# Two transformer blocks with an expert layer on one core: an earlier first search, tiles parked in the gathers' rows, another order in the mixer

## The chip, the cores and the metric

The program runs on one core of a Trainium2 chip. Five engines work side by side, each through its own list of instructions in order: TensorE (PE in the profile), VectorE (DVE), ScalarE (ACT), GpSimd (POOL), and SyncE (SP), which issues most of the transfers. They wait for each other on semaphores only. The metric is device time in microseconds of one execution, and less is better. All numbers are float32.

## The reference, cut to what matters

256 tokens of width 1024 go through two blocks. The first is a mixer (attention, and a gated linear scan in both directions), an expert layer and a small gate layer. The second is a mixer (attention, and an mLSTM) and a feed-forward layer. Most of the time lies in the expert layer:

```python
q = (ht @ w_q).reshape(T, PEER_HEADS, 2, PEER_DKEY // 2)
s = jnp.einsum('thpc,hpnc->thpn', q, sub_keys)
v1, i1 = lax.top_k(s[:, :, 0], K)                 # K = 16 of 128 keys
v2, i2 = lax.top_k(s[:, :, 1], K)
cand = (v1[..., :, None] + v2[..., None, :]).reshape(T, PEER_HEADS, K * K)
top_s, pos = lax.top_k(cand, K)                   # 16 pairs of 8 heads: 128 experts a token
idx = jnp.take_along_axis(cand_idx, pos, axis=-1) # cand_idx = i1 * 128 + i2
g = jax.nn.softmax(top_s, axis=-1)
a = jnp.einsum('thkd,td->thk', jnp.take(u, idx, axis=0), x)
w = jax.nn.gelu(a) * g
out = jnp.einsum('thk,thkd->td', w, jnp.take(v, idx, axis=0))
```

## The kernel before, in words

The 256 tokens are two blocks (b = 0, 1) of 128, one token per partition. Weights come in tiles of 2 MB through a ring of three slots (`wring`); the list `TILES` sets their order, and SP loads tile n when the product of tile n-3 is done, in that order, one after the other (L444). Products go to eight PSUM banks by the list `PLAN`. `reserved` takes a bank that another engine has emptied, `begin` counts the product in, and `wait_product` and `wait_moved` are the waits on a product and on its bank being emptied.

The order of work is written out by hand for each engine. What the change touches, in order of time:

- **Start.** SP loads block 0 of x, two small tensors, the first weight tile (`in_hf`) and block 1 of x. PE turns block 0 of the normed x (L503) and multiplies it with the whole tile (`by_block`, L596), then does the same for block 1.
- **Before the expert layer.** PE lifts both branches (`lifted`, L664: `up_att` 0 to 3, `up_hg` 0 to 3) with the transposes `g_OT` between them (L676), then makes the output product: `out0` and `out1` are the two halves of 512 columns, each for both blocks (`merged_out` L693, `by_rows` L514). DVE adds them to x (`out_added`, L1711). When block 0 is whole, ACT takes its squares (`rms`) and DVE scales it (L1440), PE turns it (`turn_query`), ACT moves it, and PE makes the query for the first head (`first_query`, L740) and its scores with the keys (`first_score`, L748); ACT copies the scores to SBUF.
- **The search.** DVE finds the 16 best of 128 keys on either side (`best_keys`), makes the 256 sums (`candidates`), finds the best 16 (`best_pairs`) and their expert numbers (`located`, L1779 writes `idx_t`). `route_first(0)` does it for the first head, `route_first(1)` for the second; later pairs of heads are cut in pieces and put between the batches by `ROUTE_AFTER`.
- **The gathers.** POOL issues one indirect DMA per slot k of 128 slots and two blocks, 256 in all (L1397). Each brings for 128 tokens one expert's row of u and of v, 8 KB a token, 1.05 MB, into one of ten rows of a ring (`pair_ring`). Gather k goes to row (k + 1) mod 10, and from k = 10 on it waits until slot k - 10 is used. Row r lies at columns 2048 r of the buffer `big`, which the mixer used before.
- **The batches.** Four slots make a batch m. DVE takes the dot products with u (`dots`, L1824), ACT the tanh of the gelu and then four diagonal matrices with the weights (`spread`, L1196), PE adds them times v (`experts`, L771). Queries of later heads are made one piece a batch (`dealt`, L715); `QUERY_FROM` says which from which batch on.
- **The mixer of the second block** (1028 to 1082 us). PE makes the scores of block 0 and 1 (`d_S`, L903), the mLSTM's `m_cols`, `m_M`, `m_S` and `m_num` (L945), the output gates (`in2_og`), the transposes of the probabilities (`d_PT`, L956) and the attended values (`d_Y`, L967). DVE and ACT work in between: `probs` and `og_tanh` on ACT, `attention_normed`, `mlstm_divided` and `mlstm_out` on DVE, which also sums the adaptive weights (`ada_sums`) where it has time.

## Time and profile before

| | us |
|---|---|
| median of 3 runs | 1347.11 (1346.61 to 1347.72) |
| the profiled execution's own time | 1346.32 |
| its span, first to last instruction | 1344.4 |
| PE busy | 1220.1 (91%) |
| DVE busy | 789.9 (59%) |
| ACT busy | 229.8 (17%) |
| POOL busy | 319.9 (24%) |

The span falls into three parts. Up to some 260 us PE works nearly without a pause. From there to some 933 us the 256 gathers run, and in most slices of the page the 16 DMA engines move about 420 GB/s. The rest is PE again.
### The profile page before, as it was taken

What the parts mean: (1) busy time and instruction counts of PE and PEld (TensorE: products, weight loads), DVE (VectorE), ACT (ScalarE), POOL (GpSimd) and SP (SyncE); (2) the same over time, 40 slices, a digit from 0 to 9 for tenths busy, and PEclk for the clock granted to TensorE, in tenths of its full rate; (3) what the DMA queues carried; (4) which work ended last, traced back from release to release, by engine and by line L of the source; (5) the groups of instructions that cost most, each with busy time, mean ns of one, the idle gap of its engine ahead of it and who ended that gap; (6) DMA issues with size and microseconds to landing.
All of it is one profiled execution on the core that took longest, in us unless ns stands there. A gap on an engine that the chain in (4) does not pass through costs nothing.

```text
span 1344.4 us, 12494 instructions
## 1 busy us (share of the span) xinstructions
PE 1220.1 (91%) x4454; PEld 735.7 (55%) x4454; DVE 789.9 (59%) x1878; ACT 229.8 (17%) x592; POOL 319.9 (24%) x276
## 2 busy tenths in 40 slices
PE   8999999978988989678889896888999999999998
PEld 7767987654544544233333342333457559888743
DVE  3766874569675877777786775656357752220101
ACT  2133210121111111112211112112201421000000
POOL 0100000124544444354545444452000000000000
PEclk9999999989989999888899999999999999999999
DMA  8441656399999999999999999999656634575540
GB/s 308 149 165 63 250 203 227 143 396 399 395 420 421 422 414 420 417 421 403 419 422 420 422 395 421 421 421 389 243 204 242 206 115 147 190 238 146 188 156 31
DMA packets 92732, 399.16 MB, mean 297 GB/s; under 512 B 6464, under 2 KB 9920, under 8 KB 59776
## 3 DMA queue, kind: packets, MB, share of 16 engines
q0 software_dynamic: 37440, 270.30, 48.9%
q1 hardware_dynamic: 55232, 128.08, 27.1%
q8 instruction: 36, 0.59, 0.2%
q14 instruction: 24, 0.20, 0.0%
HBM read 397.30 MB, written 1.06 MB: 296 GB/s over the span
## 4 chain that ended last, share of the span: by engine, by line
PE 57%; DMA 23%; DVE 14%; ACT 2%; issue 2%; POOL 1%; SPq 0%; DVEq 0%; ACTq 0%
DMA big<-in_peer_uv,idx_t 20%; PE ps L526 16%; PE ps L771 11%; PE ps L514 10%; DVE big L1824 6%; PE ps L1030 6%; PE ps L596 3%; PE ps L992 2%; PE ps L664 2%; DMA wring<-in_w_in 1%; PE ps L715 1%; DMA wring<-in_peer_wq 1%; PE ps L693 1%; PE ps L574 1%; POOL big L1397 1%
## 5 line engine op out<-in xcount | busy, mean ns | idle before, releaser
L771 PE MATMUL ps<-big,rows 128*128 128x512 f32 x1024 | 488.8, 634 | 101.4 <-ACT rows L1196 101.3
L771 PEld LDWEIGHTS ps<-big,rows 128*128 128x128 f32 x1024 | 202.6, 203 | 370.2 <-issue 370.2
L1397 POOL DMA_INDIRECT big<-in_peer_uv,idx_t x256 | 308.5, 1205 | 392.2 <-PE ps L771 332.7
L1824 DVE CUSTOM_DVE_ANT_0 big<-big 128x1024 f32<-128x1024 f32 x256 | 307.8, 1224 | 142.0 <-DMA big<-in_peer_uv,idx_t 138.9
L526 PE MATMUL ps<-big,wring 128*128 128x256 f32 x1088 | 236.8, 379 | 0.0
L526 PEld LDWEIGHTS ps<-big,wring 128*128 128x128 f32 x1088 | 206.0, 190 | 28.0 <-issue 0.5
L514 PE MATMUL ps<-wring,big 128*128 128x512 f32 (+1 forms) x336 | 140.0, 573 | 0.0
L514 PEld LDWEIGHTS ps<-wring,big 128*128 128x128 f32 x336 | 63.0, 190 | 70.5 <-issue 68.2
L1190 ACT ACTIVATE small<-small 128x4 f32<-128x4 f32 (+2 forms) x68 | 14.0, 205 | 500.6 <-DVE small L1829 491.7
L1196 ACT ACTIVATE rows<-const,small 128x128 f32<-128x128 f32 x256 | 82.2, 390 | 20.3 <-DVE small L1833 18.8
L1030 PE MATMUL ps<-wring,big 128*128 128x512 f32 x176 | 75.7, 592 | 0.0
L715 PEld LDWEIGHTS ps<-big,wring 128*128 128x128 f32 x448 | 55.4, 199 | 17.2 <-issue 9.1
L715 PE MATMUL ps<-big,wring 128*128 128x128 f32 x448 | 55.9, 282 | 7.9 <-DMA wring<-in_peer_wq 7.9
L1030 PEld LDWEIGHTS ps<-wring,big 128*128 128x128 f32 x176 | 33.4, 190 | 41.7 <-issue 41.6
L2058 DVE TENSOR_TENSOR big<-big,ps 128x512 f32<-128x512 f32 x11 | 7.6, 688 | 82.1 <-PE ps L526 74.8
L2026 DVE SCALAR_TENSOR_TENSOR big<-ps,big 128x512 f32<-128x512 f32 x8 | 5.5, 692 | 84.4 <-PE ps L1030 70.6
L1377 POOL TENSOR_TENSOR small<-small,lane 128x8 f32<-128x8 f32 x2 | 1.3, 626 | 222.9 <-DVE small L1496 222.9
L1496 DVE CUSTOM_DVE_ANT_0 wring<-wring,c_row 128x1024 f32<-128x1024 f32 x40 | 47.1, 1219 | 6.1 <-DMA wring<-in_w_ada 4.9
L596 PE MATMUL ps<-big,wring 128*128 128x128 f32 x384 | 45.1, 281 | 3.9 <-DMA wring<-in_w_in 2.9
L1075 ACT ACTIVATE big<-ps 128x512 f32<-128x512 f32 (+1 forms) x58 | 31.5, 576 | 93.3 <-PE ps L514 23.6
L596 PEld LDWEIGHTS ps<-big,wring 128*128 128x128 f32 x384 | 44.7, 197 | 4.8 <-issue 3.6
L1363 POOL DMA_DIRECT2D rows<-in_norm_ffn x1 | 0.7, 692 | 130.6 <-DVE big L1671 130.6
(246 smaller groups left out, 932.4 us busy)
## 6 DMA issues: line engine op xcount, KB each, us to landing
wring<-in_w_in SPq DMA_DIRECT2D x17, 2048.0 KB, 10.2
wring<-in_w_ada SPq DMA_DIRECT2D x10, 2048.0 KB, 7.7
wring<-in_w_gate SPq DMA_DIRECT2D x5, 2048.0 KB, 7.9
wring<-in_w_up SPq DMA_DIRECT2D x5, 2048.0 KB, 13.1
wring<-in_w_down SPq DMA_DIRECT2D x5, 2048.0 KB, 8.2
wring<-in_w_out SPq DMA_DIRECT2D x4, 2048.0 KB, 9.0
wring<-in_peer_wq SPq DMA_DIRECT2D x4, 2048.0 KB, 7.9
big<-in_peer_uv,idx_t POOLq DMA_INDIRECT x256
```

What stands on the lines that cost most here:

```text
L514: last = nc.tensor.matmul(o[:, 0:w], lhs[:, c, b * P:(b + 1) * P], wt[:, c, c0:c0 + w], start=(c == 0), stop=(c == k - 1))
L526: last = nc.tensor.matmul(o[:, c2 * S:(c2 + 1) * S], wt[:, c, n0:n0 + P], src[:, c, :], start=(c == 0), stop=(c == KD - 1))
L596: last = nc.tensor.matmul(o[:, c2 * S + b * P:c2 * S + (b + 1) * P], wt[:, c, n0:n0 + P], src[:, c, b * P:(b + 1) * P], start=(c == 0), st ...
L664: last = nc.tensor.matmul(o[:, c2 * S:(c2 + 1) * S], wt[:, c, n0:n0 + P], lhs[:, c, :], start=(c == 0), stop=(c == 3))
L715: last = nc.tensor.matmul(o[:, n * P:(n + 1) * P], wt[:, c, n * P:(n + 1) * P], h2T[b][:, c, :], start=(c == 0), stop=(c == KD - 1))
L771: last = nc.tensor.matmul(banks[h], diag[:, k % DIAGS, :], v_part[:, ring_at(k), h * 512:(h + 1) * 512], start=False, stop=(k % SLOTS == S ...
L1030: last = nc.tensor.matmul(o, gT[:, f, b * P:(b + 1) * P], wt[:, c, h * 512:(h + 1) * 512], start=(f == 0), stop=(f == FC - 1))
L1075: nc.scalar.activation(dst, bank(name, n) if src is None else src, ACT.Copy).then_inc(emptied(*name), 1)
L1196: nc.scalar.activation(diag[:, k % DIAGS, :], ident, ACT.Copy, scale=w_now[:, at_w:at_w + 1])\
L1397: pool.indirect_dma_start(pair_ring[:, ring_at(k), :], None, a["peer_uv"], bass.IndirectOffsetOnAxis(idx_t[:, k:k + 1], 0))\
L1496: last = nc.vector.tensor_tensor_reduce(w[:, c, :], w[:, c, :], c_row[:, :], 1.0, 0.0, ALU.mult, ALU.add, to[:, c:c + 1])
L1824: nc.vector.tensor_tensor_reduce(u_part[:, ring_at(k), :], u_part[:, ring_at(k), :], h_t[:, b, :], 1.0, 0.0, ALU.mult, ALU.add, a_dot[:, i ...
```

## The change

Nothing of the computation changes but its order and places.

- The first weight tile comes in two transfers (chunks 0 to 3, then 4 to 7 of the rows). PE starts on the first with column pieces 0 and 2. ACT no longer waits for the small tensor `lane` before the first squares.
- `up_att` 2 is multiplied before the transposes `g_OT` instead of after them.
- The second output tile (`out1`) and the second query tile (`peer_q1`, for block 0) are loaded into rows 6, 7 and rows 8, 9 of the gathers' ring. `peer_q1` is loaded a second time, into `wring`, for block 1. Gathers 5, 6 and 9 of the first round now wait until `out1` is done, and gathers 7 and 8 until `peer_q1` of block 0 is done. Tile `peer_q3` comes earlier in the list. The gain row of the norm moves from `rows2` to `big`.
- The scaled block 0 is handed to PE in halves. PE's order around the first query is new (below).
- The first head's search is made in two steps: the eight best pairs from the eight best keys on each side, read from PSUM, with an index step on both sides at once; then the other eight. The second head's search comes after the first batch of dots, and the second pair of heads one batch later. Scaling block 1 comes after that, too.
- `peer_q1` for block 0 precedes the first batch on PE, `peer_q2` for block 0 and the turning of block 1 follow it.
- In the mixer PE makes `m_cols` and `m_M` before the scores of block 1, `in2_og` 0 after `m_S`, and `in2_og` 1 after `m_num`; DVE and ACT follow in a like order.

TensorE between `out1` of block 0 and the first batch, before. L693 is `out0` of block 1, L503 the turning of block 0, L740 the first query, L748 the first head's scores, L514 `out1` of block 1, L715 both queries `peer_q1` and `peer_q2`, L726 their scores, L771 the first batch.

```order
L693 MATMUL ps<-wring,big 128x512 x5
L503 MATMUL ps<-const,big 128x128 x8
L693 MATMUL ps<-wring,big 128x512 x3
L740 MATMUL ps<-big,wring 128x128 x24
L748 MATMUL ps<-big 128x128 x2
L740 MATMUL ps<-big,wring 128x128 x8
L748 MATMUL ps<-big 128x128 x2
L514 MATMUL ps<-wring,big 128x512 x8
L715 MATMUL ps<-big,wring 128x128 x64
L726 MATMUL ps<-big 128x128 x4
L778 MATMUL ps<-x_t,const 128x512 x2
L771 MATMUL ps<-big,rows 128x512 x8
```

The same place in the changed kernel. L722 is the output product (from `big` where it is `out1`), L773 the turning, L782 the first query, L790 its scores. After these rows come 32 matmuls of `peer_q1` (L749), its scores and the batch; those of `peer_q2` follow the batch.

```order
L722 MATMUL ps<-wring,big 128x512 x4
L773 MATMUL ps<-const,big 128x128 x8
L722 MATMUL ps<-wring,big 128x512
L782 MATMUL ps<-big,wring 128x128 x16
L722 MATMUL ps<-wring,big 128x512
L790 MATMUL ps<-big 128x128 x2
L722 MATMUL ps<-wring,big 128x512 x2
L782 MATMUL ps<-big,wring 128x128 x16
L722 MATMUL ps<-big 128x512
L790 MATMUL ps<-big 128x128 x2
L722 MATMUL ps<-big 128x512 x7
L749 MATMUL ps<-big 128x128 x32
```

Half of the first query (16 matmuls) and two chunks of `out0` have gone behind the first scores.

VectorE after the two sums of block 0 are added, before: the search of the first head for the 16 best keys on both sides (rows 201 to 210 on this engine).

```order
L1724 MAX big<-big 128x8
L1725 MATCH_REPLACE rows<-big 128x128
L1726 MAX_INDEX big<-big 128x8
L1727 MAX big<-rows 128x8
L1728 MAX_INDEX big<-big,rows 128x8
L1724 MAX big<-big 128x8
L1725 MATCH_REPLACE rows<-big 128x128
L1726 MAX_INDEX big<-big 128x8
L1727 MAX big<-rows 128x8
L1728 MAX_INDEX big<-big,rows 128x8
```

The changed kernel from its fourth row of the search on, as far as the first eight expert numbers (L1865, row 216; the search begins at row 202).

```order
L1881 MAX_INDEX big<-big,ps 128x8
L1883 CAST big<-big 128x2x8
L1869 TENSOR_TENSOR big<-big 128x8x8
L1885 MAX big<-big 128x8
L1886 MAX_INDEX big<-big 128x8
L1857 TENSOR_SCALAR big<-big 128x8
L1858 TENSOR_SCALAR big<-big 128x8
L1859 CAST big<-big 128x2x8
L1861 TENSOR_TENSOR big<-const,big 128x128
L1863 TENSOR_TENSOR big<-big 128x128
L1864 TENSOR_REDUCE big<-big 128x2x8
L1865 SCALAR_TENSOR_TENSOR idx_t<-big 128x8
```

Before, `idx_t` is row 229, so the search is 29 instructions long. Now it is 15 long, all on eight values a side, with no MATCH_REPLACE.

ScalarE in the mixer, from the last exponentials of the mLSTM's decays, before (L1308 is `og_tanh`, L1049 a table load, L1075 a copy out of PSUM, L1056 and L1057 the norm's Ln and Exp).

```order
L1320 ACTIVATE big<-big,small 128x128
L1308 ACTIVATE big<-ps 128x512
L1049 ACT_TABLE_LOAD
L1075 ACTIVATE big<-ps 128x512 x2
L1056 ACTIVATE lnms<-ms 128x4
L1057 ACTIVATE rstd<-lnms 128x4
L1075 ACTIVATE big<-ps 128x512 x4
L1056 ACTIVATE lnms<-ms 128x4
```

The same place now (L1357 the exponentials of block 1's probabilities, L1361 `og_tanh`, L1098 and L1101 table loads, L1127 a copy).

```order
L1371 ACTIVATE big<-big,small 128x128
L1357 ACTIVATE big,small<-big,small 128x256 x8
L1361 ACTIVATE big<-ps 128x512
L1098 ACT_TABLE_LOAD
L1105 ACTIVATE lnms<-ms 128x4
L1106 ACTIVATE rstd<-lnms 128x4
L1105 ACTIVATE lnms<-ms 128x4
L1106 ACTIVATE rstd<-lnms 128x4
L1101 ACT_TABLE_LOAD
L1361 ACTIVATE big<-ps 128x512
L1127 ACTIVATE big<-ps 128x512 x6
L1098 ACT_TABLE_LOAD
```

Both norms' Ln and Exp now stand ahead of `og_tanh` 1 and of all six copies, between two table loads.

The diff, cut to its core:

```diff
-    starts = {(0, 1): 0, (0, 2): 6, (0, 3): 14, (1, 0): 20, (1, 1): 26, (1, 2): 34, (1, 3): 42}
+    starts = {(0, 1): 1, (0, 2): 6, (0, 3): 14, (1, 0): 20, (1, 1): 26, (1, 2): 34, (1, 3): 42}
...
-QUERY_FROM = {1: (1, 0), 5: (1, 1), 9: (0, 3), 14: (1, 2), 19: (1, 3)}
+QUERY_FROM = {1: (1, 0), 5: (0, 3), 9: (1, 2), 14: (1, 1), 19: (1, 3)}
...
-    t += [(f"out{i}", KD, 512, "w_out", 0, 512 * i) for i in range(2)]
-    t += [(f"peer_q{i}", KD, 512, "peer_wq", 0, 512 * i) for i in range(4)]
+    t += [("out0", KD, 512, "w_out", 0, 0)]
+    t += [(f"peer_q{i}", KD, 512, "peer_wq", 0, 512 * i) for i in (0, 2, 3, 1)]
...
-    p += [("in_g3", 1), ("g_O", 0), ("g_O", 1), ("up_att", 0), ("up_att", 1), ("g_OT", 0), ("g_OT", 1)]
-    p += [("up_att", 2), ("up_att", 3), ("up_hg", 0), ("up_hg", 1), ("up_hg", 2), ("up_hg", 3)]
+    p += [("in_g3", 1), ("g_O", 0), ("g_O", 1), ("up_att", 0), ("up_att", 1), ("up_att", 2), ("g_OT", 0), ("g_OT", 1)]
+    p += [("up_att", 3), ("up_hg", 0), ("up_hg", 1), ("up_hg", 2), ("up_hg", 3)]
     p += [("out0", 0), ("out1", 0)]
-    p += half("n2T", 0) + [("out0", 1), ("peer_q0", 0, 0), ("keys", 0, 0, 0), ("peer_q0", 0, 1), ("keys", 0, 0, 1), ("out1", 1)]
-    p += [("peer_q1", 0), ("peer_q2", 0), ("keys", 0, 1), ("keys", 0, 2)] + half("n2T", 1)
+    p += half("n2T", 0) + [("peer_q0", 0, 0), ("keys", 0, 0, 0), ("out0", 1), ("peer_q0", 0, 1), ("keys", 0, 0, 1)]
+    p += [("out1", 1), ("peer_q1", 0), ("keys", 0, 1), ("peer_q2", 0)] + half("n2T", 1) + [("keys", 0, 2)]
...
-    p += [("d_S", 1, i, g) for i in range(2) for g in range(2)]
-    p += [("m_cols",), ("m_M", 0), ("m_M", 1)] + [("m_S", h) for h in range(GH)] + [("in2_og", 1)]
-    p += [("m_num", b, i) for b in range(NB) for i in range(2)]
+    p += [("d_S", 0, i, g) for i in range(2) for g in range(2)] + [("in2_vm", 1), ("m_cols",), ("m_M", 0), ("m_M", 1)]
+    p += [("d_S", 1, i, g) for i in range(2) for g in range(2)] + [("m_S", h) for h in range(GH)] + [("in2_og", 0)]
+    p += [("m_num", b, i) for b in range(NB) for i in range(2)] + [("in2_og", 1)]
...
+                if n == 0:
+                    t = wring[:, 0:TILE].rearrange("p (c n) -> p c n", c=k)
+                    rows_ = a[src][0:D, :].rearrange("(c p) n -> p c n", p=P)[:, :, c0:c0 + w]
+                    sp.dma_start(t[:, 0:4], rows_[:, 0:4]).then_inc(first_half, 16)
+                    sp.dma_start(t[:, 4:8], rows_[:, 4:8]).then_inc(tile_landed[0], 16)
+                    sp.dma_start(x[:, 1, :], a["x"][P:S, :]).then_inc(x_landed[1], 16)
...
+                if name == "out0":
+                    wait_product(sp, "g_O", 1)
+                    sp.dma_start(out1_home, a["w_out"].rearrange("(c p) n -> p c n", p=P)[:, :, 512:1024])\
+                      .then_inc(out1_landed, 16)
+                if name == "peer_q0":
+                    wait_product(sp, "up_hg", 3)
+                    sp.dma_start(q1_home, a["peer_wq"].rearrange("(c p) n -> p c n", p=P)[:, :, 512:1024])\
+                      .then_inc(q1_landed, 16)
...
+            pe.wait_ge(first_half, 16)
+            for pieces, halves in (((0, 2), (0, 1)), ((1,), (0, 1)), ((3,), (0, 1))):
+                for c0 in halves:
+                    if c0:
+                        tile("in_hf", KD, 512)
+                    for n in pieces:
+                        o = ps[:, BANK[("in_hf", n // 2)], n % 2 * S:n % 2 * S + P]
+                        for c in range(4 * c0, 4 * c0 + 4):
+                            nc.tensor.matmul(o, first_tile[:, c, n * P:(n + 1) * P], hT[:, c, 0:P], start=(c == 0),
+                                             stop=(c == KD - 1), skip_group_check=True)
...
+            lifted("up_att", 2)
...
-            lifted("up_att", 2)
...
-                wt = tile(f"out{i}", KD, 512)
+                if i:
+                    pe.wait_ge(out1_landed, 16)
+                wt = out1_home if i else tile("out0", KD, 512)
...
+                if (name, b) == ("peer_q1", 0):
+                    pe.wait_ge(q1_landed, 16)
+                    wt = q1_home
...
             reserved("out0", 1)
-            merged_out(0, 1, range(0, 5))
-            turn_query(0)
-            begin("out0", 1)
-            merged_out(0, 1, range(5, 8)).then_inc(product_done, 1)
+            merged_out(0, 1, range(0, 4))
+            for h in range(2):
+                if h == 0:
+                    pe.wait_ge(h_half, 1)
+                else:
+                    pe.wait_ge(h_ready, 3)
+                o = begin("n2T", 0, h)
+                for c in range(4):
+                    last = nc.tensor.transpose(o[:, c * P:(c + 1) * P], h_t[:, 0, (4 * h + c) * P:(4 * h + c + 1) * P],
+                                               ident)
+                last.then_inc(product_done, 1)
+            merged_out(0, 1, range(4, 5))
             wait_turned("n2T", [0])
...
             o = begin("peer_q0", 0, 0)
             first_query(0, o)
             first_query(1, o).then_inc(product_done, 1)
-            first_query(2, reserved("peer_q0", 0, 1))
+            merged_out(0, 1, range(5, 6))
             pe.wait_ge(keys_landed, 16)
             first_score(0)
-            first_query(3, begin("peer_q0", 0, 1)).then_inc(product_done, 1)
+            begin("out0", 1)
+            merged_out(0, 1, range(6, 8)).then_inc(product_done, 1)
+            o = begin("peer_q0", 0, 1)
+            first_query(2, o)
+            first_query(3, o).then_inc(product_done, 1)
+            reserved("out1", 1)
+            merged_out(1, 1, range(0, 1))
             first_score(1)
-            by_rows("out1", hT, blocks=[1])
+            begin("out1", 1)
+            merged_out(1, 1, range(1, 8)).then_inc(product_done, 1)
...
+            score(0, 1)
             experts(0, banks)
+            query("peer_q2", 0)
+            turn_query(1)
             score(0, 2)
-            turn_query(1)
...
+                squares = at(rows2, 0, D) if (k, b) == (1, 1) else h_t[:, b, :]
+                link(nc.scalar.activation(squares, x[:, b, :], ACT.Square, accum_out=stat(ms, n)))
+                if (k, b) == (0, 0):
+                    act.wait_ge(lane_landed, 16)
...
+                    move(sc[(0, 0)][:, c, :], "keys", 0, 0, 1,
+                         src=bank(("keys", 0, 0, 1), 2 * P).rearrange("p (c t) -> p c t", c=2))
             best(0)
             act.wait_ge(x_whole, 2)
...
-            best(1)
...
+            probs(1)
+            og_tanh(0)
+            log_and_exp()
+            rsqrt(M_STAT)
+            rsqrt(M_STAT + 1)
+            exp_and_tanh()
             og_tanh(1)
...
-            wait_moved(pool, "g_O", 0)
+            pool.wait_ge(g_out, 1)
...
                 elif k % (SLOTS // PAIRS) == 0:
-                    pool.wait_ge(indexed, k // (SLOTS // PAIRS) + (2 if k else 1))
-                if ring_at(k) == 0 and k < RING:
+                    pool.wait_ge(indexed, k // (SLOTS // PAIRS) + (3 if k else 1))
+                if k < RING and ring_at(k) in (0, 6, 7):
                     wait_product(pool, "out1", 1)
+                if k < RING and ring_at(k) in (8, 9):
+                    wait_product(pool, "peer_q1", 0)
...
             out_added(1, 0)
             dve.wait_ge(gain_landed, 16)
-            scale(1, 0, gain)
-            out_added(0, 1)
+            dve.wait_ge(rstd_ready, norm_stat(1, 0) + 1)
+            for h in range(2):
+                c = slice(h * 512, (h + 1) * 512)
+                stt(h_t[:, 0, c], x[:, 0, c], stat(rstd, norm_stat(1, 0)), gain[:, c], ALU.mult, ALU.mult)\
+                    .then_inc(h_ready if h else h_half, 1)
...
-            def route_first(h):
...
+            def eight_located(first, width):
+
+                c = slice(first, first + 8)
+                ts(pos_u[:, 0, c], best_i[:, 0, c], 4, None, ALU.logical_shift_right)
...
+                h4 = hot[:, 0:2 * 8 * width].rearrange("p (s n k) -> p s n k", s=2, n=8)
...
+                link(tt(h4, h4, top_f[:, 0, :, 0:width].unsqueeze(2).to_broadcast([P, 2, 8, width]), ALU.mult))
...
+                stt(idx_t[:, c], part[:, 0, c], float(NKEYS), part[:, 1, c], ALU.mult, ALU.add).then_inc(indexed, 1)
...
+            def route_eight():
+
+                wait_product(dve, "keys", 0, 0, 0)
+                for n in range(2):
+                    link(nc.vector.max(top_v[:, n, low], first_scores[:, n, :]))
+                    last = nc.vector.max_index(top_i[:, n, low], top_v[:, n, low], first_scores[:, n, :])
+                link(last)
+                nc.vector.tensor_copy(top_f[:, 0, :, low], top_i[:, 0:2, low])
+                link(pair_sums(cand[:, 0], low, low))
+                link(nc.vector.max(best_v[:, 0, low], first_sums))
+                link(nc.vector.max_index(best_i[:, 0, low], best_v[:, 0, low], first_sums))
+                eight_located(0, 8)
...
+            route_eight()
+            out_added(0, 1)
+            route_eight_more()
+            weighed(0, 0, 0, 1, 0)
             out_added(1, 1)
-            route_first(1)
-            scale(1, 1, gain)
             for m in range(HALF_BATCHES):
                 dots(m)
                 if m == 0:
+                    route_second()
+                    scale(1, 1, gain)
+                if m == 1:
```

## Rows read from the trace of the kernel before

**Rows 1.** The page, parts 2 (GB/s in 40 slices) and 4 (the chain).

```profile
GB/s 308 149 165 63 250 203 227 143 396 399 395 420 421 422 414 420 417 421 403 419 422 420 422 395 421 421 421 389 243 204 242 206 115 147 190 238 146 188 156 31
...
DMA big<-in_peer_uv,idx_t 20%; PE ps L526 16%; PE ps L771 11%; PE ps L514 10%; DVE big L1824 6%; PE ps L1030 6%; PE ps L596 3%; PE ps L992 2%; PE ps L664 2%; DMA wring<-in_w_in 1%; PE ps L715 1%; DMA wring<-in_peer_wq 1%; PE ps L693 1%; PE ps L574 1%; POOL big L1397 1%
```

**Rows 2.** Stretches, by clock: us; busy and (instructions) per engine; PEclk, DMA share, GB/s.

```profile
260.00:270.00 10.00, 7.72 (x66) 7.29 (x64) 9.07 (x41) 1.65 (x4) 6.69 (x7) 1.00 0.83 312
290.00:320.00 30.00, 25.91 (x95) 14.15 (x93) 27.07 (x91) 5.55 (x17) 14.59 (x12) 1.00 0.98 375
330.00:340.00 10.00, 8.99 (x20) 4.09 (x21) 8.31 (x21) 2.92 (x10) 4.78 (x3) 0.83 0.87 338
```

**Rows 3.** Transfers from 200 to 262 us: GB/s in 40 slices of 1.55 us.

```profile
GB/s 0 0 11 0 0 0 53 217 414 385 408 391 389 388 384 387 388 386 381 325 20 0 0 0 0 0 0 0 0 16 296 410 399 233 0 11 0 5 0 22
```

**Rows 4.** Timeline of DVE: start us, us, line, operation, count, [idle before <-releaser].

```profile
239.83 1.28 DVE L1440 SCALAR_TENSOR_TENSOR big<-x_t,rstd,rows 128x1024 f32<-128x1024 f32 x1 [1.91 <-ACT rstd L1071]
...
251.19 0.29 DVE L1724 MAX8 big<-big 128x8 f32<-128x128 f32 x1 [5.53 <-ACT big L1075]
...
260.84 0.17 DVE L1779 SCALAR_TENSOR_TENSOR idx_t<-big 128x16 uint32<-128x16 f32 x1
...
278.45 1.23 DVE L1824 CUSTOM_DVE_ANT_0 big<-big 128x1024 f32<-128x1024 f32 x1 [1.25 <-DMA big<-in_peer_uv,idx_t]
```

**Rows 5.** Timeline of POOL: the gathers' issues.

```profile
261.30 1.03 POOL L1397 DMA_INDIRECT big<-in_peer_uv,idx_t  x1 [36.73 <-DVE idx_t L1779]
...
291.50 0.94 POOL L1397 DMA_INDIRECT big<-in_peer_uv,idx_t  x1 [17.20 <-PE ps L771]
```

**Rows 6.** Timeline of PE from `up_hg` to the first batches.

```profile
209.48 13.98 PE L664 MATMUL ps<-big 128*128 128x256 f32 x64
...
237.03 4.45 PE L693 MATMUL ps<-wring,big 128*128 128x512 f32 x10
...
260.42 7.31 PE L715 MATMUL ps<-big,wring 128*128 128x128 f32 x64
275.67 9.60 PE L715 MATMUL ps<-big,wring 128*128 128x128 f32 x64 [7.94 <-DMA wring<-in_peer_wq]
...
289.27 7.11 PE L771 MATMUL ps<-big,rows 128*128 128x512 f32 x16 [1.39 <-ACT rows L1196]
...
299.81 7.10 PE L771 MATMUL ps<-big,rows 128*128 128x512 f32 x16 [1.67 <-ACT rows L1196]
```

**Rows 7.** Timeline of ACT ahead of the first batch.

```profile
286.69 0.21 ACT L1185 ACTIVATE big<-big 128x16 f32<-128x16 f32 x1
286.92 1.28 ACT L1052 ACT_TABLE_LOAD   x1
288.21 0.20 ACT L1190 ACTIVATE small<-small 128x4 f32<-128x4 f32 x1
```

**Rows 8.** Waits of PE, 0 to 262 us: who, for whom, us in total, times, longest.

```profile
PE ps L676 <- DVE big L1679: 1.7, 2, 1.4
```

**Rows 9.** Timeline of DVE at the start.

```profile
7.75 1.29 DVE L1447 TENSOR_TENSOR big<-ps,lane 128x512 f32<-128x512 f32 x2 [0.93 <-PE ps L503]
```

**Rows 10.** Timeline of PE at the start.

```profile
11.03 8.82 PE L596 MATMUL ps<-big,wring 128*128 128x128 f32 x64 [2.88 <-DMA wring<-in_w_in]
...
21.71 7.38 PE L596 MATMUL ps<-big,wring 128*128 128x128 f32 x64 [0.99 <-DVE big L1447]
```

**Rows 11.** Timeline of PE in the mixer.

```profile
1071.17 4.59 PE L945 MATMUL ps<-big 128*128 128x129 f32 x24 [2.07 <-DVE big L1989]
...
1079.85 1.99 PE L967 MATMUL ps<-big 128*64 128x128 f32 x32 [0.45 <-ACT big L1075]
```

**Rows 12.** Timeline of DVE in the mixer.

```profile
1056.31 2.48 DVE L1957 SCALAR_TENSOR_TENSOR big<-ps,const 128x512 f32<-128x512 f32 x4 [3.30 <-PE ps L903]
...
1079.08 0.17 DVE L1425 TENSOR_SCALAR ms<-ms 128x4 f32<-128x4 f32 x1
```

**Rows 13.** Timeline of ACT in the mixer.

```profile
1077.55 2.04 ACT L1075 ACTIVATE big<-ps 128x512 f32<-128x512 f32 x4
```

116 lines of the change are left out of this document (74 added, 42 removed).

## The prediction

> **What bounds the kernel now.** I read the page's slices and chain first, then the waits of PE ahead of the gathers, then the timelines around the places that the change touches.
>
> The slices show the gathers' part: from slice 9 to slice 28 the transfers run at 389 to 422 GB/s, and the chain that ended last has 20% of its length in gathers [rows 1]. 256 gathers of 1.05 MB at 420 GB/s take 2.50 us each, 640 us together. While they saturate, no engine's work counts; what counts is when the stream starts and how often it is interrupted. It starts late: the first gather is issued at 261.30 [rows 5], and the stretch 260 to 270 moves 312 GB/s, so the full rate begins about 2.6 us into it, at 262.6. Two later stretches show where it is interrupted: against 420 GB/s, 290 to 320 loses 3.2 us (375 of 420 over 30 us) and 330 to 340 loses 2.0 (338 over 10), 5.2 together [rows 2]. Before the gathers PE runs nearly without pause, so its order sets when the scores come; and after them PE is the bound again, with waits of 2.07 and 0.45 us in the mixer [rows 11].
>
> The profiled execution took 1346.32 us, 0.8 less than the median. The sum is made against it, and 0.8 is added at the end.
>
> **First tile in halves.** PE waits 2.88 us for the tile, from 8.15 to 11.03 [rows 10]. The input that it multiplies has been written only at 7.75 + 1.29 = 9.04 [rows 9]. With the first half landed by then, PE starts at 9.2: 1.8 us. The first 64 matmuls also take 8.82 us where the second 64 take 7.38 [rows 10], which I put down to a lower clock behind the pause; with a pause of 1 us instead of 2.9 it may go, another 1.1 to 1.4. Bounds 1.8 and 3.3; I take −2.9, near the row 21.71, because the pause that is left is as long as the 0.99 us ahead of that row, behind which the rate was full. PE is the chain's engine up to the output product, so this carries through.
> The Trainium skill ("TensorE: Matmul & The Clock Gate", "What's actually happening") calls the throttled rate the default, which activity lifts. By it the start after any pause this early would be slow again, and this term would be −1.8; row 11.03 agrees, row 21.71 speaks for the other.
>
> **`up_att` 2 first.** PE waits twice, 1.7 us in all, for the gated output before `g_OT` [rows 8]. The moved product is one of those that L664 makes: four of them take 13.98 us from 209.48 [rows 6], so one takes 3.5, and it covers both waits: −1.7, bounds 0 and −1.7.
>
> **The gathers' start.** This is the large term. In the frame of before:
> - PE: chunks of the output product cost 4.45 / 5 = 0.89 us (ten rows in the trace are five matmuls) from 237.03 [rows 6]. After four chunks PE is at 240.5. DVE's scaling began at 239.83 and took 1.28 [rows 4]; its first half ends at 240.5, the second at 241.1. The eight transposes end at 241.9, the fifth chunk covers ACT's copy (242.7). Two of four query pieces (four pieces of L715 take 7.31 from 260.42, so a piece 1.83 [rows 6]) end at 246.4, one chunk at 247.2, the score product at 247.8. Before, three pieces, the copy and the copy of the scores let DVE begin at 251.19 [rows 4]. Now it reads PSUM: it begins at 247.95.
> - DVE: the old search runs from 251.19 to 260.84 + 0.17 [rows 4], 9.8 us for 29 instructions, 0.34 each. The new has 15; at that mean 5.1, but none is wider than 128 values where before half were 256 wide. A MAX over 128 is 0.29 [rows 4]; at 0.28 it is 4.2. I take 4.2: the indices are there at 252.15 instead of 261.0, the first gather is issued at 252.4 instead of 261.3: 8.9 earlier.
> - Transfers: tile `peer_q3` now takes the slot of `out0`, which is free when its last two chunks for block 1 are done, at 247.8 + 1.8 = 249.6, so the queues are busy from about 250.8 instead of 262.6: 11.8 us earlier. Both kernels then have ten gathers and one tile in front of them, 12.6 MB or 30 us, before a row has to come free.
> - Waits of POOL: gathers 0 to 4 use rows 1 to 5, free at once. Gathers 5 and 6 wait for `out1` of block 1, which PE ends at 260.7 (from 247.8: two chunks, two pieces, eight chunks of `out1`, the second scores 0.4); 7 and 8 for `peer_q1`, 7.3 later at 268.0. From 250.8 on, the tile (5 us) and gathers 0 to 4 (12.5) keep the queues busy until 268.3, two more until 273.3, so nothing runs dry. Behind POOL's wait stand only gathers.
> - The first rows come free when batch 0 has been multiplied. Gather 3 lands some 17 us after its first issue (278.45 − 1.25 − 261.3 + 0.9, [rows 4, 5]), less 2.5 for the tile that now is ahead of them instead of between: 266.6. Its dots end at 268, ACT has copies until 270.5, then a table load of 1.28 [rows 7], the tanh and four diagonals 1.9: PE starts batch 0 at 273.0. Before it started at 289.27, after 7.94 us of waiting for `peer_q2` in the middle [rows 6]. So the eleventh gather can be issued at about 276 instead of 291.5 [rows 5].
> - But batch 1 has the second head's search in front of it on DVE: 9.8 us plus 1.3 of scaling, all behind the first dots. Its diagonals come at 289.5, and PE starts it at 290 (before 299.81 [rows 6]). Between the slots freed by batch 0 and those of batch 1 the queues run dry for about 3.4 us, at 291 to 295, and some 1.2 us more goes in small gaps: 4.6 in all, against 5.2 before.
>
> The gain is 11.8 + 0.6 = 12.4 us. After 340 both are at the full rate, where the slot of a batch is freed well ahead. Bounds: by DVE and PE alone (batch 1 is 9.8 us earlier, not 12.4) −9; by the first issue with both earlier terms included, 8.9 + 4.6 = 13.5. The cost of the second `peer_q1` load, 5 us of transfer, is nothing net: a tile of 2.1 MB that was loaded ahead of the gathers' start (`peer_q3` now, `out1` and `peer_q1` before they start) has left the stretch. If that cover fails it costs 5 us.
> What is late next in this stretch is DVE, with both searches.
>
> **Loads before it.** Before, the transfers ahead of `out0` run from about 210 us (slice 7) to 230 at 388 GB/s [rows 3]: keys, `out0`, `out1` and `peer_q0`, 1 + 3 x 2.1 MB = 7.3 MB. The same four tensors come now, `out1` into another place and behind the same `out0`; only `peer_q1` is new, after `up_hg` 3 at 223.5 [rows 6], needed at 260. `out1` is needed at 230 and is third of the four: (1 + 4.2) MB at 388 GB/s is 13.4 us, landed near 224. 6 us to spare: nothing.
>
> **The mixer.** PE makes `m_M` first, so DVE waits less than its 3.30 us before the second score block [rows 12] and begins it at about 1053. Its row of work from 1056.31 to 1079.08 + 0.17 [rows 12] is 22.9 us; 2.3 of `m_M` and 1.5 of waits leave it, two adaptive sums of 1.15 come in. It ends at 1074.6. But ACT now does both norms' Ln and Exp (0.45) and a second table load (1.28, [rows 7]) ahead of `og_tanh` 1 (0.6) and the copies of d_PT, whose last four take 2.04 us from 1077.55 [rows 13]. So these begin at 1078.1 and end at 1080.3, and the attended values, at 1079.85 before [rows 11], start at 1080.4: +0.5. PE is idle longer ahead of it (4 us, before 2.07 [rows 11]), so the products behind may run slower, 0 to 1.2. I take +1.0, bounds −0.5 and +2.2.
> The Trainium skill ("ScalarE: Activation LUTs", "What ACT_TABLE_LOAD costs") adds to each load of about 1283 ns a drain of about 1380 ns. Here the row before the load ends at 286.90, the load starts at 286.92, and the next activation at 288.21 [rows 7]: no drain is seen. By the page's rule this term would be +2.4 and the total an estimated 1332.5; I go by the row.
>
> **The sum.** −2.9 − 1.7 − 12.4 + 1.0 = −16.0: 1330.3 for a profiled execution, 1331.1 for the median.
>
> **The rivals.**
> - Consumption sets the early pace. DVE has to do 11 us of search behind the first dots and PE two queries between batches 0 and 1; if each is a few us longer than I have it, the ring of ten is full and the queues stand. Then the stage gains what batch 1 gains, 9.8, less a delay of the first dots by about one gather (2.5 us) that shares the queues with the tile: 7 in place of 12.4: 1331.1 + 5.4 = 1336.5. For it: the interruptions are all in 290 to 340 [rows 2], where batches 0 to 4 are. Against: the ring holds 30 us of transfer.
> - Only the front gains. The gathers start earlier but their end is set by something after the first stretch, so that the stage ends where it did: −2.9 − 1.7 + 1.0 leave 1343.5. For it: three slices between 12 and 27 show under 415 GB/s [rows 1]. Against: the rest are at 420 and leave no slack to give back.
> - The gain is larger. The gaps of 290 to 340 vanish altogether, another 4.6: 1326.5.
> - Slower than before: the tile `out1` lands late. The queues bring the four tensors and, from 223.5, `peer_q1`, at less than I have, and PE stands in front of the second half of the output product; the scores, the search and the whole stream of gathers move by as much. It decides from the point at which that delay eats the 16 us, `out1` landing at 246 in the frame of before. If the queues gave no more than the 143 GB/s of slice 8 [rows 1] and shared it evenly among the 7.3 MB, the last would land 51 us after 208, at 259, 29 late: 1360. For it: slices 5 to 8 show 143 to 250 GB/s [rows 1]. Against: those are what was asked for; when four tensors were asked for at once it was 388 [rows 3].
>
> **How the numbers follow.** Forecast (1327.5 to 1334.5) 0.60; consumption 0.20 (1334.5 to 1340); only the front 0.07; larger 0.08; slower, the late tile, 0.05. The range 1326.5 to 1338.5 holds the first, most of the second and half of the fourth, 0.8. A measurement of this kernel tells 0.2%, 2.7 us, from no change: faster takes all of the first, second and fourth and half of the third, 0.92; same 0.03; slower 0.05.
>
> **What would show it.** PE's first products start near 9.2 at full clock; no wait at `g_OT`; the first MAX near 243 and the first gather near 248 (both 4.6 earlier than the frame above); `out1` and `peer_q1` without a wait; batch 0 on PE near 268, batch 1 near 285; a gap in the transfers of about 3 us in front of batch 1's slots; the rate of 420 GB/s from 335 on, and 256 gathers over 16 us earlier; the attended values 0.5 us later against their stage. The prediction is wrong if batch 1 comes after 290, if the queues stand more than 8 us in total before 335, or if PE waits for `out1`.

## The result, and the profile after

| | before | changed |
|---|---|---|
| median of 4 runs, us | 1347.41 (1346.61 to 1349.61) | 1332.34 (1332.32 to 1332.90) |
| the profiled execution's own time | 1346.32 | 1332.32 |
| its span | 1344.4 | 1330.5 |

The ratio is 0.9885 (95% interval 0.9869 to 0.9902): faster by 1.15%. 1331.1 was forecast. Measured again later, beside other runs of before, the same kernel gave 0.9880 (0.9861 to 0.9899). The kernel before had medians from 1347.41 to 1350.37 us in the four series of this document, so kernels of different series are compared by their ratios. One execution among those below stands apart, 2851.89 us in the kernel with the earlier table load: its ratio leaves it out, and the median of its other four is 1331.44.

The page of the changed kernel, its GB/s in 40 slices and its chain, answering to [rows 1]:

```profile
GB/s 312 184 133 64 253 200 321 291 373 406 418 421 420 421 423 415 416 420 410 418 421 422 397 405 422 421 420 339 231 190 252 206 127 156 191 223 143 190 158 32
...
DMA big<-in_peer_uv,idx_t 20%; PE ps L543 18%; PE ps L818 12%; PE ps L531 8%; DVE big L1941 6%; PE ps L1079 6%; PE ps L613 3%; PE ps L691 2%; PE ps L722 2%; PE ps L1041 2%; PE ps L749 2%; PE ps L591 1%; POOL big L1454 1%; DMA wring<-in_w_in 1%; ACT rows L1247 1%
```

The stream of gathers is as full as before and its share of the chain is still 20%. It begins and ends about half a slice earlier: the first gather falls into slice 8 in both kernels (291 GB/s, before 143). Slice 7 (321 GB/s, before 227) holds weight tiles, of which two more now come there: SP issues `peer_q1` at 218.01 and `peer_q2` at 218.42.

PE at the start, for [rows 10]:

```profile
8.85 7.66 PE L628 MATMUL ps<-big,wring 128*128 128x128 f32 x64 [0.99 <-DVE big L1504]
...
18.37 7.38 PE L613 MATMUL ps<-big,wring 128*128 128x128 f32 x64 [0.99 <-DVE big L1504]
```

The pause is 0.99 us instead of 2.88, the 64 products take 7.66 instead of 8.82, and the second run starts at 18.37 instead of 21.71: 3.34 us. PE at `g_OT` (L704, the old L676), which no longer waits for DVE, at `up_hg`, at batches 0 and 1 and behind the last batch, for [rows 8 and 6]:

```profile
199.68 1.04 PE L704 MATMUL ps<-const,big 128*128 128x128 f32 x8
...
204.00 13.98 PE L691 MATMUL ps<-big 128*128 128x256 f32 x64
...
267.68 7.10 PE L818 MATMUL ps<-big,rows 128*128 128x512 f32 x16 [3.00 <-ACT rows L1247]
...
285.35 7.11 PE L818 MATMUL ps<-big,rows 128*128 128x512 f32 x16 [1.57 <-ACT rows L1247]
...
927.40 3.67 PE L898 MATMUL ps<-wring,big 128*128 128x512 f32 x8 [0.51 <-DMA wring<-in_w_in]
```

`up_hg` starts at 204.00 (before 209.48), 5.48 earlier: 3.34 from the start and 2.14 from the two waits at `g_OT`. The first search on DVE, for [rows 4]:

```profile
242.37 0.30 DVE L1880 MAX8 big<-ps 128x8 f32<-128x128 f32 x1 [6.60 <-PE ps L790]
...
244.04 0.43 DVE L1885 MAX8 big<-big 128x8 f32<-128x256 f32 x1
...
246.49 0.17 DVE L1865 SCALAR_TENSOR_TENSOR idx_t<-big 128x8 uint32<-128x8 f32 x1
```

The search takes 4.29 us from 242.37 to 246.66, where it was 9.8. One of its rows is 256 wide (L1885, the `cand` buffer whose unused part is filled with a large negative number), which I had not seen. POOL, for [rows 5]:

```profile
246.95 1.03 POOL L1454 DMA_INDIRECT big<-in_peer_uv,idx_t  x1 [27.86 <-DVE idx_t L1865]
...
255.21 0.94 POOL L1454 DMA_INDIRECT big<-in_peer_uv,idx_t  x1 [2.24 <-PE ps L722]
...
262.35 0.94 POOL L1454 DMA_INDIRECT big<-in_peer_uv,idx_t  x1 [4.40 <-PE ps L749]
...
287.58 0.94 POOL L1454 DMA_INDIRECT big<-in_peer_uv,idx_t  x1 [11.58 <-PE ps L818]
```

The first issue is 14.35 us earlier. The two waits for the parked tiles (2.24 and 4.40 us) stop nothing: the transfers run at the full rate from 250 to 280, and stand only in the next stretch, for [rows 2]:

```profile
250.00:280.00 30.00, 27.00 (x153) 19.38 (x152) 22.38 (x74) 6.04 (x14) 12.23 (x12) 1.00 1.02 421
280.00:290.00 10.00, 8.43 (x45) 5.73 (x44) 8.34 (x33) 3.54 (x9) 1.64 (x2) 1.00 0.72 278
290.00:310.00 20.00, 18.32 (x66) 9.99 (x65) 18.63 (x61) 2.96 (x10) 10.28 (x9) 1.00 0.99 391
```

Against 420 GB/s, 280 to 290 loses 3.4 us, 290 to 310 another 1.4: 4.8, where 4.6 was forecast. ACT ahead of batch 0 and of batch 1, for [rows 7]:

```profile
265.34 1.28 ACT L1101 ACT_TABLE_LOAD   x1
266.63 0.20 ACT L1241 ACTIVATE small<-small 128x4 f32<-128x4 f32 x1
...
283.81 0.60 ACT L1127 ACTIVATE big<-ps 128x512 f32<-128x512 f32 x1 [0.27 <-PE ps L760]
284.31 0.20 ACT L1241 ACTIVATE small<-small 128x4 f32<-128x4 f32 x1
```

And the mixer, PE and then ACT, for [rows 11 and 13]:

```profile
1012.06 1.91 PE L926 MATMUL ps<-const,big 128*128 128x128 f32 x16
...
1061.89 5.83 PE L1016 MATMUL ps<-big 128*64 128x128 f32 x48 [3.73 <-ACT big L1127]
...
1068.37 7.03 PE L1041 MATMUL ps<-wring,big 128*128 128x512 f32 x16
```

```profile
1058.46 0.20 ACT L1105 ACTIVATE lnms<-ms 128x4 f32<-128x4 f32 x1 [5.55 <-DVE ms L1482]
...
1058.92 1.28 ACT L1101 ACT_TABLE_LOAD   x1
...
1060.71 3.04 ACT L1127 ACTIVATE big<-ps 128x512 f32<-128x512 f32 x6
```

PE waits 3.73 us in one piece and then makes the attended values in 5.83 us; before they took 1.09 and 1.99. From the first transposes of the mixer (L926) to the output product (L1041) it is 56.3 us, before 54.0 (1028.26 to 1082.26).

The account, by the starts of rows that both kernels have: start of the kernel to the second run of 64 products −3.34; `g_OT` −2.14; from there to the end of the batches −10.9 (the product behind them starts at 927.40, before 943.76); from there to the mixer +0.2; the mixer +2.3. Together −13.9, the difference of the spans.

### The profile page after: what moved, and what is told of

Its sections match the earlier page's. It is cut to its first block, busy times and chain, and to the rows that moved or that the text cites. A ratio compares the mean times of both kernels' runs of the same rounds, so it can differ in the third digit from the quotient of the medians.

```text
span 1330.5 us, 12510 instructions
## 1 busy us (share of the span) xinstructions
PE 1211.0 (91%) x4454; PEld 730.4 (55%) x4454; DVE 791.2 (59%) x1886; ACT 231.9 (17%) x593; POOL 321.6 (24%) x276
## 4 chain that ended last, share of the span: by engine, by line
PE 60%; DMA 21%; DVE 14%; issue 2%; ACT 2%; POOL 1%; DVEq 0%; SPq 0%
DMA big<-in_peer_uv,idx_t 20%; PE ps L543 18%; PE ps L818 12%; PE ps L531 8%; DVE big L1941 6%; PE ps L1079 6%; PE ps L613 3%; PE ps L691 2%; PE ps L722 2%; PE ps L1041 2%; PE ps L749 2%; PE ps L591 1%; POOL big L1454 1%; DMA wring<-in_w_in 1%; ACT rows L1247 1%
## 5 line engine op out<-in xcount | busy, mean ns | idle before, releaser
L818 PE MATMUL ps<-big,rows 128*128 128x512 f32 x1024 | 482.4, 627 | 107.3 <-ACT rows L1247 107.2
L818 PEld LDWEIGHTS ps<-big,rows 128*128 128x128 f32 x1024 | 199.9, 200 | 371.8 <-issue 371.8
L543 PEld LDWEIGHTS ps<-big,wring 128*128 128x128 f32 x1088 | 206.0, 190 | 28.0 <-issue 0.5
L531 PE MATMUL ps<-wring,big 128*128 128x512 f32 (+1 forms) x304 | 126.0, 571 | 0.0
L1241 ACT ACTIVATE small<-small 128x4 f32<-128x4 f32 (+2 forms) x68 | 13.9, 205 | 502.3 <-DVE small L1946 502.3
L531 PEld LDWEIGHTS ps<-wring,big 128*128 128x128 f32 x304 | 57.0, 190 | 62.8 <-issue 61.0
L1079 PEld LDWEIGHTS ps<-wring,big 128*128 128x128 f32 x176 | 33.4, 190 | 41.7 <-issue 41.6
L749 PEld LDWEIGHTS ps<-big,wring 128*128 128x128 f32 x384 | 46.0, 192 | 9.1 <-issue 9.1
L749 PE MATMUL ps<-big,wring 128*128 128x128 f32 x384 | 46.3, 275 | 0.0
L1127 ACT ACTIVATE big<-ps 128x512 f32<-128x512 f32 (+1 forms) x57 | 31.0, 582 | 73.9 <-PE ps L531 23.8
L613 PE MATMUL ps<-big,wring 128*128 128x128 f32 x320 | 36.3, 275 | 1.0 <-DVE big L1504 1.0
L613 PEld LDWEIGHTS ps<-big,wring 128*128 128x128 f32 x320 | 36.0, 192 | 1.7 <-DVE big L1504 1.2
```

The lines of the kernel that those rows point to most:

```text
L531: last = nc.tensor.matmul(o[:, 0:w], lhs[:, c, b * P:(b + 1) * P], wt[:, c, c0:c0 + w], start=(c == 0), stop=(c == k - 1))
L543: last = nc.tensor.matmul(o[:, c2 * S:(c2 + 1) * S], wt[:, c, n0:n0 + P], src[:, c, :], start=(c == 0), stop=(c == KD - 1))
L613: last = nc.tensor.matmul(o[:, c2 * S + b * P:c2 * S + (b + 1) * P], wt[:, c, n0:n0 + P], src[:, c, b * P:(b + 1) * P], start=(c == 0), st ...
L749: last = nc.tensor.matmul(o[:, n * P:(n + 1) * P], wt[:, c, n * P:(n + 1) * P], h2T[b][:, c, :], start=(c == 0), stop=(c == KD - 1))
L818: last = nc.tensor.matmul(banks[h], diag[:, k % DIAGS, :], v_part[:, ring_at(k), h * 512:(h + 1) * 512], start=False, stop=(k % SLOTS == S ...
L1079: last = nc.tensor.matmul(o, gT[:, f, b * P:(b + 1) * P], wt[:, c, h * 512:(h + 1) * 512], start=(f == 0), stop=(f == FC - 1))
```

## The experiments

All are the changed kernel with one edit, unless said otherwise; "ratio" is to the kernel before of the same series. With the landing of the first tile, kernels that are the same up to the first gather issue it 0.1 to 0.7 us later than the changed kernel's profiled execution did (one, below, is 1.5 us late at the start). Rows are compared after taking that shift off where it isn't what is tested.

**The first tile whole again** (L454 and L619 as before):

```diff
-                    sp.dma_start(t[:, 0:4], rows_[:, 0:4]).then_inc(first_half, 16)
-                    sp.dma_start(t[:, 4:8], rows_[:, 4:8]).then_inc(tile_landed[0], 16)
...
+            by_block("in_hf", 0, hT)
```

> The changed kernel with its first weight tile in one transfer again, and PE on it in the order of before; all else as changed. Theory: the halving gave back the wait (from 8.15 to 9.04, the end of the turned input) and the lower clock behind it, 3.3 us at the row where the second run of 64 products starts, and nothing later hides it: 3.3 us slower than the changed kernel, 1335.6. PE's first products start at 11.0 after a wait of 2.9 and take 8.8. Rival, by the clock rule: the pace at the start does not hang on the pause, so only the start moves: 2.0 us slower, 1334.3, and the 64 products take 7.7 as in the changed kernel.

Measured: 1339.74 us, ratio 0.9921 (0.9903 to 0.9940). By the times that is 7.4 us more than the changed kernel and more than either theory says; by the ratios it is 4.9, and their intervals do not exclude 3.3. PE at the start, at the first batch and at the second:

```profile
12.26 8.87 PE L608 MATMUL ps<-big,wring 128*128 128x128 f32 x64 [4.34 <-DMA wring<-in_w_in]
...
22.99 7.38 PE L608 MATMUL ps<-big,wring 128*128 128x128 f32 x64 [0.99 <-DVE big L1489]
...
272.30 10.03 PE L803 MATMUL ps<-big,rows 128*128 128x512 f32 x16 [3.00 <-ACT rows L1232]
...
292.90 7.11 PE L803 MATMUL ps<-big,rows 128*128 128x512 f32 x16 [1.57 <-ACT rows L1232]
```

The tile landed at 12.26 here (11.03 in [rows 10]), so the second run starts 4.6 us later than in the changed kernel, and the 64 products take 8.87 again, at a granted clock of 0.50 in 12 to 14 us (before, too; 1.00 in the changed kernel). In the twelve profiled executions of kernels with the tile in halves PE stood idle 0.99 to 1.90 us ahead of these products, seven of them once more for 0.25 to 0.59 us, for the second half, and the products took 7.6 to 7.7 us. So the slow pace does come with the long waits (2.88 and 4.34 us), and halving is worth 3.3 to 4.6 in these executions, by how late the tile lands. What I had not expected is at 272.30: batch 0 takes 10.03 us where the changed kernel had 7.10, at a granted clock of 0.66 in 270 to 280. That makes batch 1 7.6 us later, not 4.6. That the late front brought this lower clock is not shown: batch 0 also ran slower in executions whose front was not late (last section).

**`up_att` 2 behind `g_OT` again:**

```diff
             lifted("up_att", 1)
-            lifted("up_att", 2)
             for b in range(NB):
...
+            lifted("up_att", 2)
             lifted("up_att", 3)
```

> The changed kernel with up_att 2 behind the transposes g_OT again. Theory: PE waits twice there again, 0.3 and 1.4 us, plus some 0.4 of restarts, and nothing behind takes it back: the output product and the first gather come 2.1 us later, total 2 us slower than the changed kernel in the same call's frame (1334.3). Rival: the stream of gathers absorbs it, since batch 0 waits 3 us for ACT: less than 0.5 us.

Measured: 1336.83 us, ratio 0.9912 (0.9896 to 0.9929). PE's waits up to 262 us, and its batch 0:

```profile
PE ps L628 <- DMA wring<-in_w_in: 2.5, 2, 1.9
PE ps L703 <- DVE big L1736: 1.7, 2, 1.4
```

```profile
271.32 8.70 PE L818 MATMUL ps<-big,rows 128*128 128x512 f32 x16 [3.00 <-ACT rows L1247]
```

Both waits are back, 1.7 us, and the first gather is 3.6 us later, 1.5 of which come from late halves of the first tile in this execution (2.5 us of waits for them). The 2.1 us are there; batch 0 again ran slower (8.70) and added 1.6. The span is 5.2 us longer than the changed kernel's, all of the 3.6 and the 1.6, so the rival, that the stream absorbs it, is out.

**The gathers wait for all sixteen pairs of the first head:**

```diff
-                if k in (TOPK // 2, TOPK):
-                    pool.wait_ge(indexed, 2 * k // TOPK + 1)
+                if k in (0, TOPK):
+                    pool.wait_ge(indexed, 2 + k // TOPK)
```

> The changed kernel with the gathers held until all sixteen pairs of the first head are found, instead of the first eight: the first issue is at about 254.1 instead of 246.95, 7.2 us later. Nothing is left out. Theory: the tile peer_q3 keeps the queues busy to about 251, so the stream loses some 4 us there, and of these the gap that the changed kernel has anyway at 283 to 287 absorbs a part, since batch 1 is held by DVE: fourth gather 2.5 to 3 us later, batch 1 on PE 2.5 to 3 later, total +2.5 to +4 (1335 to 1336.5). Rival: every us of a later first gather is a us of the total, +7 (1339.5). Third: +0 to 1, if what DVE does between batches 0 and 1 sets the pace.

Measured: 1338.41 us, ratio 0.9915 (0.9899 to 0.9932). PE's batches 0 and 1:

```profile
271.81 9.57 PE L818 MATMUL ps<-big,rows 128*128 128x512 f32 x16 [6.40 <-ACT rows L1247]
...
291.94 7.10 PE L818 MATMUL ps<-big,rows 128*128 128x512 f32 x16 [1.57 <-ACT rows L1247]
```

The first issue is 254.75, 7.1 later after a shift of 0.7 (taken at the first MAX). Batch 0 is 3.4 later by the same count, near the theory's 2.5 to 3, but takes 9.57 us behind a wait of 6.40, and batch 1 is 5.9 later. The total is 4 us more by the ratios, the upper end of the theory, and 6 by the times: not a us for a us, but 3.4 of a late batch plus 2.5 of clock. This run alone does not tell slots from bytes: from 240 to 270 us the transfers moved 139, 193 and 406 GB/s against 161, 418 and 423, a loss of 6.3 us.

**`peer_q2` ahead of batch 0 again:**

```diff
-            experts(0, banks)
             query("peer_q2", 0)
+            experts(0, banks)
```

> The changed kernel with the 32 products of peer_q2 for block 0 put ahead of the first batch on PE again. Batch 0 starts about 7 us later (275 instead of 267.7), so gathers 10 to 13 are issued 7 us later. Theory: batch 1, which DVE holds with the second head's search until 285, decides when slots come free; the queues have work until 276 without gather 10, so at most 1 us is lost there, and it comes out of the gap at 283: total 0 to +1 (1332.3 to 1333.3). That would mean that the 16 us by which batch 0 came earlier is worth next to nothing. Rival: the stream loses what batch 0 loses, +7 (1339).

Measured: 1334.03 us, ratio 0.9880 (0.9862 to 0.9898), by the ratio the same as the changed kernel, by the times 1.7 more. PE's batches 0 and 1:

```profile
272.28 7.03 PE L818 MATMUL ps<-big,rows 128*128 128x512 f32 x16
...
285.05 8.80 PE L818 MATMUL ps<-big,rows 128*128 128x512 f32 x16 [3.97 <-ACT rows L1247]
```

Batch 0 is 4.0 later (7 were expected; PE no longer stands idle ahead of it), batch 1 0.9 earlier (both after the shift of 0.6). But batch 1 took 8.80 us here and ended 0.8 later, and so does the last batch (0.9). Four us of batch 0 are thus worth 0.9 at most, and that may be the clock.

**Batch 1 ahead of `peer_q2`, the second search behind its dots:**

```diff
             experts(0, banks)
+            experts(1, banks)
             query("peer_q2", 0)
...
                 if m == 0:
-                    route_second()
                     scale(1, 1, gain)
                 if m == 1:
+                    route_second()
                     weighed(0, 0, 1, 2, 1)
```

> The changed kernel with batch 1 ahead of the peer_q2 products on PE, its diagonals ahead of the exponentials of the second head and of the copies on ACT, and the second head's search behind the dots of batch 1 on DVE (scaling of block 1 stays ahead of them). Theory: the 4 us that the transfers stand at 283 to 287 come from batch 1 waiting at 285 behind peer_q2 and its copies; it now starts at about 276 to 277, gathers 14 to 17 are issued from 279 on (16 and 17 when the indices are there, about 286), and the stream does not stand before batch 2: 3.5 to 4.5 us faster than the changed kernel (1328 to 1329). Rival: DVE's search of 10 us sets the pace wherever it stands, and the gap only moves in front of batch 2: within 1 us of 1332.

Measured: 1332.92 us, ratio 0.9873 (0.9858 to 0.9888), no gain; the rival holds. PE's batches (0 and 1 in one row, then 2), and the transfers:

```profile
268.22 15.62 PE L818 MATMUL ps<-big,rows 128*128 128x512 f32 x32 [3.00 <-ACT rows L1249]
...
296.01 7.10 PE L818 MATMUL ps<-big,rows 128*128 128x512 f32 x16 [1.28 <-ACT rows L1249]
```

```profile
280.00:290.00 10.00, 10.00 (x66) 7.85 (x66) 9.24 (x41) 0.21 (x1) 2.80 (x3) 1.00 1.01 419
290.00:300.00 10.00, 8.71 (x51) 6.32 (x51) 9.24 (x32) 3.65 (x9) 0.98 (x2) 1.00 0.71 284
```

The transfers do not stand in 280 to 290 (419 GB/s), they stand in 290 to 300 (284): the gap moved from in front of batch 1 to in front of batch 2. The two batches took 15.62 us, 1.4 more than twice 7.10, batch 2 starts 0.6 later than in the changed kernel, and gather 18 is issued at 298.24 (changed kernel 297.14, with a shift of 0.5). DVE was busy for 8.3 to 9.4 of each 10 us from 280 to 320 in both kernels.

**Tile `peer_q3` 11 us later:**

```diff
+                if name == "peer_q3":
+                    wait_product(sp, "out1", 1)
```

> The changed kernel with the tile peer_q3 loaded only when out1 is done (255 instead of 244). The stream then begins with gathers at 248.5 and loses the 3.3 us before them. Theory of the prediction (bytes: an earlier start of the stream is a gain one for one): 3.3 us slower, 1335.6. Rival (consumption sets the early pace): batch 0 waits for ACT's copies and table load and not for gathers, so it stays at 267.7, the 5 us of the tile fall into the 4 us that the transfers stand at 283 to 287: 0 to +1, 1332.3 to 1333.3, and the gap there shrinks to about 1 us.

Measured: 1333.11 us, ratio 0.9887 (0.9872 to 0.9903), the same as the changed kernel. The transfers, and batches 0 and 1:

```profile
280.00:290.00 10.00, 8.43 (x57) 6.77 (x57) 6.69 (x28) 3.54 (x9) 0.58 (x1) 1.00 1.01 416
290.00:300.00 10.00, 9.33 (x35) 5.10 (x34) 9.24 (x33) 1.48 (x5) 4.91 (x5) 1.00 0.93 347
```

```profile
267.82 8.80 PE L820 MATMUL ps<-big,rows 128*128 128x512 f32 x16 [3.00 <-ACT rows L1249]
...
287.19 7.10 PE L820 MATMUL ps<-big,rows 128*128 128x512 f32 x16 [1.57 <-ACT rows L1249]
```

240 to 250 moved 24 GB/s here, 161 in the changed kernel. What the stream lost there it made up in 280 to 290, 416 GB/s. Batch 0 starts where it did; 1.7 us of slower clock in it (8.80) make batch 1 later by 1.7 and the end of the batches by 2.2. By the medians the total is 0.8 up at most, and the profiled execution is only 0.1 longer because its mixer was short (54.35 us, 56.31 in the changed kernel). What the tile costs is seen against the kernel with the copies of d_PT ahead (below), which is the changed kernel up to the mixer and whose batch 0 took 8.80, too:

```profile
268.36 8.80 PE L818 MATMUL ps<-big,rows 128*128 128x512 f32 x16 [2.99 <-ACT rows L1247]
```

From the first gather to the end of the batches it is 682.74 us there and 682.65 with the late tile. Transfers that begin 3.3 us earlier are worth nothing as such.

**ACT's table load ahead of two copies:**

```diff
+            exp_and_tanh()
             query_out(0, 1)
             scores_out(0, 1)
...
-            exp_and_tanh()
             spread(0)
```

> The changed kernel with ACT's table load for exponential and tanh ahead of the copies of the second query and its scores instead of behind them. Theory: dots of batch 0 end at 264.6, ACT reaches the tanh only at 266.6 because of the load of 1.28; now at 265.4, and since DVE's second search, PE's batch 0, peer_q2 and batch 1 all stand behind that tanh, batches 0 and 1 come 1.3 us earlier, and so do all freed slots: 1.0 to 1.3 us faster, 1331.2. Rival: what is won is lost in the stream's gaps, 0.

Measured: 1332.09 us, ratio 0.9870 (0.9851 to 0.9888), against 0.9885 and 0.9880 for the changed kernel: the right sign, within the intervals. PE's batches 0 and 1:

```profile
266.78 7.10 PE L818 MATMUL ps<-big,rows 128*128 128x512 f32 x16 [1.62 <-ACT rows L1247]
...
284.45 7.11 PE L818 MATMUL ps<-big,rows 128*128 128x512 f32 x16 [1.57 <-ACT rows L1247]
```

With a shift of 0.5, batches 0 and 1 are 1.4 earlier, and the end of the batches 1.3. In the second combination (below), the same kernel up to the mixer, the batches are 1.4 earlier again but their end only 0.4, and two executions of kernels that share the changed order up to there differ by 1.1: the gain at the batches is shown, what is left of it at the end is not. The front of this stage is a chain: tanh of batch 0 on ACT, batch 0, `peer_q2`, its copies, batch 1.

**The mixer in the order of before** (all of its PE, ACT and DVE order):

```diff
-            scored(1)
             pe.wait_ge(qkm_ready, 1)
...
-            probs(1)
-            og_tanh(0)
-            log_and_exp()
-            rsqrt(M_STAT)
-            rsqrt(M_STAT + 1)
-            exp_and_tanh()
             og_tanh(1)
+            log_and_exp()
```

> The changed kernel with the second block's mixer (PE, ACT, DVE and the list of products there) in the order of before. Theory: the changed order costs 2.07 us between the first transposes of the mixer and the transposes of the merged heads (54.0 us before, 56.1 after), by a wait of 3.7 us ahead of the attended values and the lower clock behind it: 2.1 us faster than the changed kernel, 1330.3, PE waits 2.1 and 0.45 us again. Rival: the two orders cost the same and the difference came from the clock of that one execution, within 0.5 us of 1332.3. Third: the new order of the mixer brings something behind it (the merged heads of block 1, the norms) that this one loses: slower than 1332.3.

Measured: 1333.12 us, ratio 0.9875 (0.9855 to 0.9895). PE's waits behind the batches:

```profile
PE ps L995 <- DVE big L2109: 2.1, 1, 2.1
PE ps L532 <- DMA wring<-in_w_in: 1.6, 1, 1.6
...
PE ps L1017 <- ACT big L1128: 0.5, 1, 0.5
```

The stage took 55.85 us, 0.5 less than in the changed kernel. In it are 1.6 us of waiting for `in2_og`, issued 13.0 us ahead of its use; before it was issued 12.95 ahead and there was no wait. Without that wait the stage is 54.3, near the 54.0 of before. In the nine profiled executions with the new order the stage took 54.35 to 56.49 us, 56.31 in the middle, so the new order costs some 2 us in most of them. Why the tile took longer in this execution stays open, and the timing alone does not tell 2 us from 0.5.

**The copies of d_PT ahead, one table load instead of three** (the second norm comes between the copies of block 0 and those of block 1):

```diff
             og_tanh(0)
+            og_tanh(1)
             log_and_exp()
             rsqrt(M_STAT)
-            rsqrt(M_STAT + 1)
-            exp_and_tanh()
-            og_tanh(1)
...
+            rsqrt(M_STAT + 1)
...
-            log_and_exp()
```

> The changed kernel with ACT in the mixer in another order: og_tanh 1 ahead of the table load, then the norm of block 0, the two copies of d_PT for block 0, the norm of block 1 and the four other copies; the second and third table loads fall away. Theory: PE waited 3.7 us for these copies, which stood behind the norm of block 1 (ready at 1058.4), a load of 1.28 and a tanh, and it then ran at 1.2 GHz; now the copies start when PE's transposes are done (1058.2) and end at 1061.2 instead of 1063.75: PE's wait falls to about 1.5 in two pieces, the attended values run at full clock, 2.5 to 4.5 us faster than the changed kernel (1328 to 1330). Rival: the merged heads of DVE, ready at 1062.4, or the tile of the output product hold PE next: at most 1 us faster.

Measured: 1330.44 us, ratio 0.9858 (0.9843 to 0.9873), against 0.9880 (0.9861 to 0.9899) in the same series; the intervals overlap. PE:

```profile
1061.77 1.09 PE L1016 MATMUL ps<-big 128*64 128x128 f32 x16 [0.84 <-ACT big L1127]
1064.20 1.99 PE L1016 MATMUL ps<-big 128*64 128x128 f32 x32 [1.34 <-ACT big L1127]
...
1066.61 7.03 PE L1041 MATMUL ps<-wring,big 128*128 128x512 f32 x16
```

The wait is 0.84 + 1.34 us instead of 3.73, and the products run in 1.09 and 1.99, as before the change. The output product follows 8.5 us after the start of the transposes (1058.15 to 1066.61). In the changed kernel it was 13.0, and 10.2 in its repeated execution (1057.09 to 1067.24), where the products ran faster: 1.7 to 4.5 us, and the two ratios give 3.0. The three profiled executions with this order of ACT took 51.78, 51.79 and 53.41 us for the whole stage; none of the nine with the changed order is below 54.35, so the gain is clear of their spread. In this execution the 8.80 us of batch 0 take part of it back: its end of the batches is 2.3 later.

**Two combinations.** The first joins the last edit with that of the late second search, the second joins it with the early table load.

> Both of the foregoing edits in one kernel. They lie in different stages, so the gains should add: 6 to 9 us faster than the changed kernel, 1323.5 to 1326.5. If the early one is given back later in the gathers (the stream being bound by its bytes), it is that of the mixer alone, 1328 to 1330.

> The early table load and the other order of ACT in the mixer together: 1.2 + 2 us faster than the changed kernel, 1329.0; below 1328.5 it would beat every kernel so far.

Measured: 1329.49 us, ratio 0.9852 (0.9838 to 0.9865) for the first, which is the mixer's gain alone, and 1327.91 us, ratio 0.9840 (0.9825 to 0.9855), for the second. PE of the second, at batch 0 and at the attended values:

```profile
266.37 7.10 PE L818 MATMUL ps<-big,rows 128*128 128x512 f32 x16 [1.61 <-ACT rows L1247]
```

```profile
1060.11 1.09 PE L1016 MATMUL ps<-big 128*64 128x128 f32 x16 [0.84 <-ACT big L1127]
```

It beats both kernels: 1.6% below before, and 0.4% below the changed one by the two ratios of 0.9880 and 0.9840 (of two series, so about that).

**The changed kernel again.**

> The changed kernel once more, so that it and the kernels of this call stand beside the same runs of before. Expected 0.9885 of the kernel before, as in its first timing, and the same trace within 1 us at every row.

Measured: 1332.15 us, ratio 0.9880. For the first thirty gathers its rows stand 0.3 us off the first execution's, and so does the end of the batches, though between them issues differ by up to 3.5 us and the last is 1.8 later. The span is 1.1 shorter. The bound of 1 us at every row was too tight: the mixer took 55.08 us, with the attended values in 4.5.

**Which row the end of the gathers' part follows.** In us later than in the changed kernel (minus: earlier), after the shift; "end" is the first product behind the last batch.

| kernel | first gather | batch 0 | batch 1 | batch 2 | end |
|---|---|---|---|---|---|
| `peer_q2` ahead of batch 0 | 0 | 4.0 | −0.9 | −0.1 | 0.9 |
| batch 1 ahead of `peer_q2` | 0 | 0 | about −9 | 0.6 | 0.2 |
| tile `peer_q3` later (batch 0 in 8.80) | 0 | 0 | 1.7 | 1.7 | 2.2 |
| copies of d_PT ahead (batch 0 in 8.80) | 0 | 0 | 1.7 | 1.7 | 2.3 |
| table load ahead | 0 | −1.4 | −1.4 | −1.4 | −1.3 |
| all sixteen pairs first | 7.1 | 3.4 | 5.9 | 5.9 | 5.5 |
| mixer as before, the same up to here | 0 | 0 | 0 | 0 | 1.1 |
| `up_att` 2 late (shift not taken off) | 3.6 | 3.6 | 5.2 | 5.2 | 5.4 |
| first tile whole (shift not taken off) | 4.6 | 4.6 | 7.6 | 7.6 | 8.8 |

The end follows batch 2 to within 1.3 us, and the row "mixer as before" shows that the same order differs by 1.1 between executions. It follows neither the first gather nor batch 0, and batch 1 only where batch 2 comes with it.

## Why the prediction was right, and where it was not

- **First tile** −2.9: measured −3.34, of the two parts that it names (2.18 of start, 1.16 of pace), just over the outer bound. By the Trainium skill ("TensorE: Matmul & The Clock Gate", "What's actually happening") the default state is throttled and activity releases it. That any pause so early brings the default back, which gave −1.8, was my own reading of that sentence. It was too small here: the products took 7.66 us behind a pause of 0.99, 8.82 behind 2.88 and 8.87 behind 4.34.
- **`up_att` 2** −1.7: measured −2.14, since each wait also cost some 0.2 us around it.
- **The first issue** 13.5 earlier: 14.35. The search was 4.29 (4.2), although one row is wider than I said. The waits for the parked tiles and the loads before them cost nothing, as forecast, although behind `up_hg` 3 two tiles are loaded and not only `peer_q1`.
- **Batches**: 0 near 268.4 and 1 near 285.4 were forecast; 267.68 and 285.35. The gap of 3.4 and the sum of 4.6 us lost: 3.4 and 4.8.
- **The step that failed is the reason given for the −12.4**: "the queues are busy from about 250.8 instead of 262.6: 11.8 us earlier", taken as a gain one for one. Transfers that begin 3.3 us later cost nothing (`peer_q3` 11 us later), 4 us of batch 0 are worth 0.9 at most, and a gap closed in front of batch 1 opens in front of batch 2. What sets the pace to 300 us is the use of the slots: ACT's tanh, batch 0, `peer_q2` and its copies on one side, DVE with both searches and the dots, busy 92 to 94% from 290 to 320, on the other. Batch 1 is 14.5 us earlier than before: 5.5 from the front and 9.0 from this stage, where PE's wait of 7.94 us for the tile `peer_q2` is gone, too [rows 6]. The other 1.9 came after it. Before, the transfers lost 2.0 in 330 to 340, and now 0.2; that this is the reason was not tested. The number held by luck in part: 12.4 by transfers and 9.8 by batches lie on either side of the 10.9 measured. The mechanism is that of the rival that I called consumption, without its delay of 2.5 us, which did not come because batch 0 waited for ACT and not for a gather.
- I also said that DVE's second search holds batch 1. DVE's work for the tanh of batch 1 was done at 283.40, and ACT began that tanh at 284.31, behind the copies of `peer_q2` and of its scores (the last from 283.81). So the copies hold it, but by 0.9 us only; next in line is DVE.
- **The mixer** +1.0: the account gives +2.3, just over the outer bound of +2.2. The wait was as drawn (4 us, measured 3.73). The term that was mis-sized is the clock behind it: 0.5 of the +1.0, bound 1.2, and 2.7 came, 5.83 us for products of 3.1. In the repeated execution they took 4.5, so this term varies.
- **The drain**: in the changed kernel a load starts at 265.34, 0.01 us behind the copy before it, and the next activation at 266.63, a load of 1.28 and nothing else. By the Trainium skill ("ScalarE: Activation LUTs", "What ACT_TABLE_LOAD costs") there would be 1.38 more. No load in these traces shows it. The total that the prediction works out with it, 1332.5, is nearer to the measured 1332.34 than its own, but by accident: the mixer's +2.3 is the clock behind the wait and not a drain.
- The gathers' part came out 1.5 us smaller than forecast, the front 0.9 larger, the mixer 1.3 worse, 0.2 between them: the profiled execution took 1332.32 us against 1330.3. The median, 1332.34, is nearer to its forecast of 1331.1 because the 0.8 us that was added for it did not come. The total is a sum of errors of both signs.
- No run puts the parked tiles back or moves the second search alone. What these parts of the change are worth by themselves is read from rows only.

## What to carry to other kernels

Where a stream of transfers goes through a ring of slots, ask which instruction frees the slot that the stream will next run dry for, and follow that one back; here neither the start of the stream nor the first batch was worth anything beyond that. A wait of some us in front of PE cost its length and, in some executions and not in others, 1.6 to 2.9 us of lower clock in the batch behind it. Before a gain of that size is believed, look whether the clock of the two traces is the same. And a table load or a wait for a late input does not belong in front of copies that another engine is waiting for: the mixer's three stages with the copies ahead are all shorter than the nine without, by 0.9 us at least.

## What was not expected of the hardware

Batch 0 is 16 matmul instructions behind 3.0 us of idle PE (2.99 or 3.00) in seven profiled executions. It took 7.10, 7.11, 7.11 and 8.80 us in four that are the same kernel up to this row (changed, changed again, mixer as before, copies of d_PT ahead), and 8.70, 8.80 and 10.03 in three others (`up_att` late, `peer_q3` late, whole tile). The granted clock in the stretch 270 to 280 was 1.00, 1.00, 1.00 and 0.90 in the four and 0.83, 0.91 and 0.66 in the three. The same instructions behind the same wait thus ran at either pace: the wait directly in front is not all that sets the clock behind it. What else does was not isolated.
